# Diagonal blocks copied by ScalarE, block sums in another order, a buffer cleared after both lots of transfers

## The reference

```python
x = x + 0.5 * _swiglu(_rmsnorm(x, ffn1_norm[l]), ffn1_w_gate[l], ffn1_w_up[l], ffn1_w_down[l])
h = _rmsnorm(x, mix_norm[l])          # the mixer: one projection, three attentions, gates, w_out
...
x = x + (g[:, :, 0] * y_a + g[:, :, 1] * y_b + g[:, :, 2] * y_c) @ w_out[l]
x = x + 0.5 * _swiglu(_rmsnorm(x, ffn2_norm[l]), ffn2_w_gate[l], ffn2_w_up[l], ffn2_w_down[l])
```

## Time and profile before

| | us |
|---|---|
| median of 3 runs | 1170.22 |
| lowest and highest | 1169.62, 1171.65 |
| the profiled execution | 1170.92 |
| its span, first to last instruction | 1169.2 |
| busy TensorE / weight loads / DVE | 1144.6 / 933.1 / 881.7 |
| busy ScalarE / GpSimd | 612.7 / 289.0 |
| mean granted clock of TensorE | 0.993 of full speed |

### The profile page before, as it was taken

The page is one execution under the profiler, slowest core; times in us unless marked ns, Lnnn a source line. Parts: engine busy times, 40 slices in busy tenths (PEclk is TensorE's granted clock), DMA queues, the critical chain, the costliest instruction groups (busy, mean ns, idle before and its releaser), DMA issues. The chain is left out here.

```text
span 1169.2 us, 15632 instructions
## 1 busy us (share of the span) xinstructions
PE 1144.6 (98%) x5477; PEld 933.1 (80%) x5477; DVE 881.7 (75%) x1274; ACT 612.7 (52%) x789; POOL 289.0 (25%) x573
## 2 busy tenths in 40 slices
PE   9999999999999999999999999999899999999995
PEld 7877888887778888878887888888777788878884
DVE  6677877789978577688677678677798686777874
ACT  6345645457864544455454555453677545454632
POOL 2322350151000013323322231503410000323341
PEclk9999999999999999999999999999899999999998
DMA  8976665795333587656677766658843355777561
GB/s 290 310 257 200 194 225 189 220 263 182 109 115 141 185 289 253 222 179 215 219 231 252 237 198 225 204 183 220 243 145 109 109 180 188 258 263 233 162 218 43
DMA packets 173199, 238.45 MB, mean 204 GB/s; under 512 B 19936, under 2 KB 117968, under 8 KB 173136
## 3 DMA queue, kind: packets, MB, share of 16 engines
q1 hardware_dynamic: 146720, 222.23, 57.8%
q0 software_dynamic: 16128, 11.44, 3.9%
q10 hardware_dynamic: 10288, 4.00, 1.3%
HBM read 221.86 MB, written 1.05 MB: 191 GB/s over the span
## 5 line engine op out<-in xcount | busy, mean ns | idle before, releaser
L637 DVE TENSOR_TENSOR wlo<-raw,whi 128x2048 fp32r<-128x2048 f32 (+2 forms) x195 | 426.7, 2193 | 169.2 <-ACT whi L1334 148.7
L1334 ACT ACTIVATE whi<-raw 128x2048 fp32r<-128x2048 f32 (+2 forms) x195 | 358.6, 1841 | 224.8 <-issue 115.7
L1630 PE MATMUL ps<-whi,ht_hi 128*128 128x512 f32 (+1 forms) x1064 | 416.7, 392 | 0.6 <-DVE wlo L637 0.3
L1632 PE MATMUL ps<-whi,ht_lo 128*128 128x512 f32 (+1 forms) x1064 | 411.9, 387 | 0.0
L1631 PE MATMUL ps<-wlo,ht_hi 128*128 128x512 f32 (+1 forms) x1064 | 411.5, 387 | 0.0
L534 POOL DMA_DIRECT2D act_blocks<-act_blocks x352 | 173.1, 500 | 412.1 <-DVE act_blocks L707 409.8
L1630 PEld LDWEIGHTS ps<-whi,ht_hi 128*128 128x128 f32 x1064 | 200.7, 189 | 41.1 <-ACT whi L1334 1.0
L1632 PEld LDWEIGHTS ps<-whi,ht_lo 128*128 128x128 f32 x1064 | 200.4, 188 | 41.1
L1631 PEld LDWEIGHTS ps<-wlo,ht_hi 128*128 128x128 f32 x1064 | 200.7, 189 | 38.8
L1630 PE MATMUL ps<-whi,at_hi 128*128 128x512 f32 x304 | 120.2, 395 | 5.3 <-DVE at_lo L713 5.2
L1631 PE MATMUL ps<-wlo,at_hi 128*128 128x512 f32 x304 | 118.5, 390 | 0.0
(11 more groups left out here) (231 smaller groups left out, 1224.6 us busy)
## 6 DMA issues: line engine op xcount, KB each, us to landing
raw<-in_ffn_w_down_dram SPq DMA_DIRECT2D x88, 512.0 KB, 4.4
raw<-in_w_in_dram SPq DMA_DIRECT2D x88, 512.0 KB, 4.5
raw<-in_ffn_w_gate_dram SPq DMA_DIRECT2D x77, 512.0 KB, 4.2
raw<-in_ffn_w_up_dram SPq DMA_DIRECT2D x77, 512.0 KB, 5.3
T_raw<-in_ffn_w_gate_dram SPq DMA_DIRECT2D x16, 512.0 KB, 6.2
T_raw<-in_ffn_w_up_dram SPq DMA_DIRECT2D x16, 512.0 KB, 6.6
raw<-in_w_out_dram SPq DMA_DIRECT2D x16, 512.0 KB, 4.3
act_blocks<-act_blocks POOLq DMA_DIRECT2D x352, 16.0 KB, 4.1
```

The lines of the kernel that those rows point to most:

```text
L637: nc.vector.tensor_tensor(wlo[:, n, 0:w], raw[:, n, 0:w], whi[:, n, 0:w].bitcast(F32), ALU.subtract).then_inc(lo_done, 1)
L1334: nc.scalar.activation(whi[:, n, 0:w], raw[:, n, 0:w], ACT.Copy).then_inc(hi_done, 1)
L1630: nc.tensor.matmul(o, xh, wh, start=start, stop=False)
L1632: return nc.tensor.matmul(o, xl, wh, start=False, stop=stop)
```

## The change

- BY_ACT is now (3,0), (3,1), (3,2), (2,0), (2,3): five transfers as before. BY_POOL is the rest of the blocks with a other than q: seven.
- The four diagonal blocks are copied by ScalarE, with one activation each (`keep_act`), behind its five transfers. at_hi waits for these too, on a new semaphore.
- GpSimd has a drain between the loop over steps 1 to 7 and steps 8 to 10.
- In the mixer GpSimd issues both lots before it waits for the first and clears cmpm.
- On DVE, side sums (steps 1, 2) and block sums (steps 4, 5, 6) run ahead of the conversion of slab 3i+4; at_lo follows that conversion at once; side rests, the third block sum and the first sum rest come behind at_lo.
- On ScalarE the high part of T2, third in the order, is made behind at_hi of step 6.

```diff
-        BY_ACT = [(3, 0), (3, 1), (3, 2), (3, 3), (2, 3)]
-        BY_POOL = [(a, q) for a in range(4) for q in range(4) if (a, q) not in BY_ACT]
+                eng.wait_ge(act_kept, (r * (NSTEP - 1) + i) * 4)
+
+        BY_ACT = [(3, 0), (3, 1), (3, 2), (2, 0), (2, 3)]
+        BY_POOL = [(a, q) for a in range(4) for q in range(4) if a != q and (a, q) not in BY_ACT]
...
                     convert(l, s0 + 3 * i + 3, w)
+                    if i < 3:
+                        side_sums(l, f, i - 1)
+                    if 4 <= i < 7:
+                        block_sum(l, f, {4: 0, 5: 1, 6: 3}[i])
                     if i < PAIR - 1:
                         convert(l, s0 + 3 * i + 4)
-                    if i < 3:
-                        side_sums(l, f, i - 1)
+                        act_rest(l, f, i)
+                    else:
+                        sum_rest(l, f, 1)
+                        sum_rest(l, f, 2)
                     if i == 3:
                         for m in range(4):
                             side_rest(l, f, m)
-                    for m in {4: (0,), 5: (1, 2), 6: (3,)}.get(i, ()):
-                        block_sum(l, f, m)
-                    for m in {6: (0,), 7: (1, 2)}.get(i, ()):
-                        sum_rest(l, f, m)
-                    if i < PAIR - 1:
-                        act_rest(l, f, i)
+                    if i == 5:
+                        block_sum(l, f, 2)
+                    if i == 6:
+                        sum_rest(l, f, 0)
...
                     cross_act(pool, l, f, i, BY_POOL, act_crossed_rest)
+                pool.drain()
                 for i in range(PAIR, NSTEP):
...
                 cross(l, 0)
+                cross(l, 1)
                 pool.wait_ge(crossed[0], (l + 1) * 256)
                 nc.gpsimd.memset(cmpm[:, :, :, :], 0.0).then_inc(cmpm_zero, 1)
-                cross(l, 1)
...
+            def keep_act(i):
+
+                blocks_in, blocks_out = act_set(i)
+                for q in range(4):
+                    nc.scalar.activation(blocks_out[32 * q:32 * q + 32, P * q:P * q + P],
+                                         blocks_in[32 * q:32 * q + 32, P * q:P * q + P], ACT.Copy).then_inc(act_kept, 1)
...
                     cross_act(eng, l, f, i, BY_ACT, act_crossed)
+                    keep_act(i)
                     if i < PAIR - 1:
                         convert(l, s0 + 3 * i + 4)
                     if i == 3:
                         side_round(l, f)
-                    for m in {5: (0,), 6: (1, 2), 7: (3,)}.get(i, ()):
-                        sum_round(l, f, m)
+                    if 5 <= i:
+                        sum_round(l, f, {5: 0, 6: 1, 7: 3}[i])
                     if i < PAIR - 1:
                         act_round(l, f, i)
+                    if i == 6:
+                        sum_round(l, f, 2)
```

More of the change, by code:

```diff
@@ L311, in build @@
         act_turned = sem("act_turned")
+        act_kept = sem("act_kept")
         act_crossed = [sem(f"act_crossed{n}") for n in range(3)]
@@ L1455, in ffn @@
                 cross_act(eng, l, f, PAIR, BY_ACT, act_crossed)
+                keep_act(PAIR)
                 convert(l, s0 + OUT_SLAB + 1)
                 cross_act(eng, l, f, PAIR + 1, BY_ACT, act_crossed)
+                keep_act(PAIR + 1)
                 silu(l, f, last, False)
@@ L1461, in ffn @@
                 cross_act(eng, l, f, last, BY_ACT, act_crossed)
+                keep_act(last)
                 act_round(l, f, PAIR + 1)
```

## The result

| | before | after |
|---|---|---|
| median, us (4 runs each) | 1169.92 | 1151.38 |
| lowest and highest | 1167.55, 1171.65 | 1151.05, 1151.98 |
| the profiled execution | 1170.92 | 1151.98 |
| its span | 1169.2 | 1150.2 |

The changed kernel is faster: ratio 0.9843, 95% interval 0.9825 to 0.9861. The forecast was 1157.0 us with a range from 1153.0.

The account below looks back on a forecast made before the run. It took the time to be TensorE's matmuls plus its gaps: 1170.92 - 10.5 + 1.7 - 4.4 - 0.3 = 1157.4 us, lowered to the runs' median and called 1157, with a range of 1153 to 1164.5.

Parts of the forecast that it names:

- gaps before at_lo and bt_lo: Four feed-forward layers: TensorE's gaps at weight loads for the down products all go, -10.5 us.
- new gap at the fourth sum: Step 7 of each feed-forward layer: ScalarE's uncovered copies open a gap of 0.43 us, +1.7 us in all.
- mixer of layer 1 (wait and clock): Before L2007: earlier second lot shortens the wait by 2.0 us, and avoiding half clock saves 2.4: -4.4 us.
- mixer of layer 0: Before L2007 in layer 0: 0.3 us of the 0.46 us wait goes, -0.3 us.
- GpSimd's drain: Between steps 7 and 8 of each feed-forward layer: the added drain lies in a pause and changes nothing, 0 us.
- The copies: ScalarE's four diagonal copies take 0.8 us a step, hidden in steps 1 to 6 but not in step 7.
- Rival C: Chain to the fourth sum: ScalarE's copies are dear, slower from 1.04 us each, 1174.3 us at 1.3; chance 0.07.
- the weakest point: Mixer of layer 1: the clock stays up at 1.5 us of waiting, worth 2.4 us.
- Rivals A and D: First, mixer gains nothing, 1161.5 us, chance 0.18; second, early second lot delays first lot and loads, 1166 us, chance 0.05.

Follow-up runs that it names:

- e1: The changed kernel without GpSimd's added drains, all else as changed: 1156.54 us, ratio 0.9890 to the kernel before.
- e3: The kernel before with one added GpSimd drain, in the last feed-forward layer only: 1164.65 us, ratio 0.9950.
- e5: The kernel before with only the buffer clearing moved behind both lots in both mixers: 1165.34 us, ratio 0.9966.
- e2: The kernel before with GpSimd's four drains alone, one in each feed-forward layer: 1158.35 us, ratio 0.9905.
- e8: The kernel before with seven transfers from GpSimd and ScalarE's four copies, old order, no drains, clearing between the lots: 1165.50 us, ratio 0.9969.
- e6: The changed kernel with the buffer cleared between the lots again: 1151.55 us, ratio 0.9854 to the kernel before.

## Why the prediction was wrong

By terms, forecast against measured, in us of the span:

| term of the sum | forecast | measured |
|---|---|---|
| gaps before at_lo and bt_lo | -10.5 | -9.3 |
| new gap at the fourth sum | +1.7 | +3.2 |
| mixer of layer 1 (wait and clock) | -4.4 | -6.0 |
| mixer of layer 0 | -0.3 | -0.1 |
| GpSimd's drain | 0 | -6.7 |

1170.92 - 9.3 + 3.2 - 6.0 - 0.1 - 6.7 = 1152.0, and the profiled execution was 1151.98.

**The step that failed is "GpSimd's drain ... Zero".** I asked what the added instruction could cost, found it covered, which was right (7.1 to 9.5 us, all inside the pause), and didn't ask what it could give: the end is 6.7 us shorter, some 5.2 by the added drains (e1) and 1.4 by the fewer transfers. The answer was in the trace of before, in rows that I didn't read: the last matmuls and outputs end seven microseconds ahead of the span's end, and only GpSimd's drain is left. The sum began at TensorE's gaps and took the tail for granted, though the prediction says itself that the time is TensorE's work plus its gaps, which leaves out what stands behind its last matmul. With this term alone the forecast would have been near 1150.3, and its range would have held the time.

**The gaps before at_lo** all went, as forecast. The size was off for two reasons that lie against each other. My list left out one gap of step 5, 1.10 us in the first layer: it is 17 gaps and 11.5 us at the loads, with bt_lo 12.3. And a gap at a weight load overstates the loss, since loads run ahead of the matmuls: the 0.98 us at the fourth sum's load are 0.74 between the matmuls' starts. In starts, 9.3 us went.

**The copies.** 0.8 us for four was too little: 1.33. I had let each start before the end of the one before it, as the 2048-element ones do (524.37 to 526.20 is 1.83, with records of 1.92). The short ones don't: each has a record of 0.31 and starts 0.33 behind the last. The Trainium skill ("ScalarE: Activation LUTs", What ACT_TABLE_LOAD costs) gives back-to-back activations an overlap of 93 ns; the trace agrees for the long copies and not for these. The step's frame held: 4 x 0.33 - 0.37 gives a gap of 0.96, and 0.98 was read in three layers. Rival C was the same mechanism with a price of 1.04; it is a third of that.

**The mixer.** The wait went altogether, not by 2 us, and the clock stayed up, which I had called the weakest point. Right in kind, 1.6 us too small: the whole wait went where 2 us were taken. Of the 6.0 us about 2.5 are the clock, and these depend on which execution of the kernel before was profiled (e3). Rivals A and D fall with e5: moving the clearing alone gave 4.5 us, though the lot and the loads ran side by side. What I had noted of GpSimd only as "a break in issuing of 1.6 us was seen" was itself part of the cause: e2 and e8, which remove the break and leave the clearing, lose the wait too.

**The parts are not a sum.** For the mixer three edits are each enough (e2, e5, e8), so each looks worthless once another is in (e6). For at_lo two edits are each of little use (2.3 and 1.1 us) and together give 9.3. My sum came out near for the pair only because I had counted both at once; that the order's edit opens a gap at step 4, which only the seven transfers cover, was not in it.

What stays open: why GpSimd breaks off where it does after the first 128 transfers, why its drain is bounded, and why the clock falls behind some waits of 3 us and not behind others.

## What to carry to other kernels

Read the last ten microseconds of a span by engine, the drains and semaphores too, before the gaps in the middle: what stands behind the last matmul counts once, but in full. Ask of every added instruction both what it costs and what it takes from a later one. And when an edit frees a chain by one wait, look for the engine that is second on it, here the ScalarE and VectorE order behind the transfers; experiments one part at a time show it, and a sum of parts doesn't.

## Of the hardware

- GpSimd's last drain, 15 us or more behind its last issue, cost 0.67 us and 0.082 us for each of its own transfers since the drain before (0, 21, 33 transfers), and 9.6 and 11.0 us behind 344 and 504. Directly behind 21 transfers a drain took 2.9 to 5.3 us. Paid in a pause of over 20 us of that engine, it cost nothing.
- Without drains GpSimd broke off its issuing three or four times for 1.3 to 2.3 us, first behind 128 transfers; with a drain in each layer at most two breaks of 0.2 to 0.3 us were left.
- Behind a wait of TensorE of 3.1 to 3.5 us the clock fell to half for 3.4 or 6.8 us, or not at all (e3).
- Four copies of 32 partitions x 128 elements cost ScalarE 1.3 us everywhere and GpSimd 1.3 to 4.6 us, by the step.
